# A one-core hybrid decoder layer on TensorE: twelve multiplications of ones put into a wait of the first tile, and the outputs of a tile's first two chunks formed together

## The reference

```python
h = rmsnorm(x, g_pre_mix)
z, q, k, v, glow, og = jnp.split(h @ w_in, SPLIT_IDX, axis=-1)
gk = jax.nn.log_sigmoid((glow @ w_gk2 + b_gk2).astype(jnp.float32)) / GLA_GATE_NORMALIZER
pool_out, pool_new = pool_mixer(z, pool_buf, start, w_pool, pool_scale)
gla_out, gla_new = gla_mixer(q, k, v, gk, og, gla_state, gla_norm)
mix = jnp.concatenate([pool_out.astype(x.dtype), gla_out.astype(x.dtype)], axis=-1) @ w_o
x = x + rmsnorm(mix, g_post_mix)
f, conv_new = conv_ffn(rmsnorm(x, g_pre_ffn), conv_buf, w_up, w_conv, b_conv, w_down)
x = x + rmsnorm(f, g_post_ffn)
x = x + (p.astype(x.dtype) @ w_ple) * jax.nn.sigmoid(x @ w_ple_gate)
```

```python
o_inter = jnp.einsum('bhtd,bhdv->bhtv', qc * jnp.exp(b), S)
o = o_inter + jnp.einsum('bhts,bhsv->bhtv', A, vc)
...
o = rmsnorm(o, gla_norm)
o = o.transpose(0, 2, 1, 3).reshape(B, L, GLA_VDIM) * jax.nn.silu(og.astype(f32))
```

## Time and profile before

| | us |
|---|---|
| median of 3 runs | 2523.79 (2523.52 to 2526.18) |
| the profiled execution, its own time | 2522.07 |
| its span in the trace | 2520.3 |
| PE busy | 2500.1 (99%) |
| DVE busy | 1592.6 (63%) |
| ACT busy | 1296.7 (51%) |
| POOL busy | 177.5 (7%) |
| TensorE clock granted, mean | 0.998 |

### The profile page before, as it was taken

How to read it: one execution, slowest core, us unless ns; L and a number is a source line. 1 busy time by engine, 2 the same in 40 slices (tenths; PEclk the granted TensorE clock), 3 DMA queues, 4 the chain that set the end, 5 groups by cost and what they waited for, 6 DMA issues and landing times.

```text
span 2520.3 us, 40462 instructions
## 1 busy us (share of the span) xinstructions
PE 2500.1 (99%) x16224; PEld 2432.9 (97%) x16224; DVE 1592.6 (63%) x2523; ACT 1296.7 (51%) x1989; POOL 177.5 (7%) x508
## 2 busy tenths in 40 slices
PE   9999999999999999999999999999999999999998
PEld 8889999989999999999999999999999999999998
DVE  6778765666665456666545666655566664667865
ACT  5455554564444456444445644444564444566554
POOL 4201000100000010000001000000100000010000
PEclk9999999999999999999999999999999999999999
DMA  8435556444444644544464544346454434656565
GB/s 249 133 127 165 172 150 234 143 159 147 153 127 124 223 144 166 153 154 123 126 217 152 167 150 152 122 130 215 151 167 151 142 123 129 204 186 209 190 181 182
DMA packets 120473, 409.08 MB, mean 162 GB/s; under 512 B 12896, under 2 KB 22496, under 8 KB 119776
## 3 DMA queue, kind: packets, MB, share of 16 engines
q1 hardware_dynamic: 120288, 406.51, 50.2%
HBM read 383.56 MB, written 22.89 MB: 161 GB/s over the span
## 4 chain that ended last, share of the span: by engine, by line
PE 97%; DVE 2%; ACT 1%; issue 1%; DMA 0%; DVEq 0%; POOL 0%; ACTq 0%; POOLq 0%
PE G L1628 29%; PE G L1630 29%; PE G L1629 29%; PE X L1674 2%; PE G L1907 1%; PE G L1908 1%; PE G L1909 1%; PE X L1624 1%; PE X L1732 1%; PE X L1738 0%; DVE w_lo L1128 0%; PE X L1791 0%; PE G L1870 0%; PE X L1653 0%; PE X L1717 0%
## 5 line engine op out<-in xcount | busy, mean ns | idle before, releaser
L1628 PE MATMUL G<-h_hi,w_hi 128*128 128x384 f32 (+2 forms) x3072 | 997.8, 325 | 6.0 <-DVE w_lo L1128 3.1
L1630 PE MATMUL G<-h_lo,w_hi 128*128 128x384 f32 (+2 forms) x3072 | 987.9, 322 | 0.0
L1629 PE MATMUL G<-h_hi,w_lo 128*128 128x384 f32 (+2 forms) x3072 | 987.8, 322 | 0.0
L725 ACT ACTIVATE w_hi<-stage 128x1024 fp32r<-128x1024 f32 (+1 forms) x505 | 524.1, 1038 | 416.2 <-DMA stage<-in_w_up_units_dram 243.5
L1128 DVE TENSOR_TENSOR w_lo<-stage,w_hi 128x1024 fp32r<-128x1024 f32 (+1 forms) x505 | 604.9, 1198 | 160.7 <-ACT w_hi L725 160.1
L1628 PEld LDWEIGHTS G<-h_hi,w_hi 128*128 128x128 f32 x3072 | 579.4, 189 | 14.4 <-DVE w_lo L1128 4.4
L1629 PEld LDWEIGHTS G<-h_hi,w_lo 128*128 128x128 f32 x3072 | 579.6, 189 | 1.5
L1630 PEld LDWEIGHTS G<-h_lo,w_hi 128*128 128x128 f32 x3072 | 579.3, 189 | 0.0
L1628 PE MATMUL G<-y_hi,w_hi 128*128 128x384 f32 (+2 forms) x1056 | 342.6, 324 | 0.0
L1630 PE MATMUL G<-y_lo,w_hi 128*128 128x384 f32 (+2 forms) x1056 | 339.4, 321 | 0.0
L1629 PE MATMUL G<-y_hi,w_lo 128*128 128x384 f32 (+2 forms) x1056 | 339.3, 321 | 0.0
(11 more groups left out here) (213 smaller groups left out, 2700.0 us busy)
## 6 DMA issues: line engine op xcount, KB each, us to landing
stage<-in_w_up_units_dram SPq DMA_DIRECT2D x264, 512.0 KB, 3.6
w_lo<-kept_lo SPq DMA_DIRECT2D x107, 512.0 KB, 4.7
stage<-in_w_down_units_dram SPq DMA_DIRECT2D x96, 448.0 KB, 3.3
w_whole<-in_w_in_units_dram SPq DMA_DIRECT2D x72, 512.0 KB, 3.8
stage<-in_w_o_units_dram SPq DMA_DIRECT2D x48, 512.0 KB, 3.5
stage<-in_w_down_units_dram SPq DMA_DIRECT2D x48, 512.0 KB, 3.5
w_whole<-in_w_gate_units_dram SPq DMA_DIRECT2D x35, 512.0 KB, 3.8
stage<-in_w_in_units_dram SPq DMA_DIRECT2D x24, 512.0 KB, 4.4
```

The costliest lines, as they stand in the source:

```text
L725: act.activation(w_hi[s][:, 0:parts, :], whole[:, 0:parts, :], ACT.Copy).then_inc(hi_made, 1)
L1628: pe.matmul(ps[:, 0:w], l_hi, r_hi[:, 0:w], start=start, stop=False)
L1629: pe.matmul(ps[:, 0:w], l_lo, r_hi[:, 0:w], start=False, stop=False)
L1630: return pe.matmul(ps[:, 0:w], l_hi, r_lo[:, 0:w], start=False, stop=stop)
```

## The change

Two edits. First, PE no longer forms chunk 0's output after unit in 13; it forms chunks 0 and 1 together after unit in 14, and ACT copies both out at its step 15. Chunk 2 stays where it was. Second, in tile 0 twelve multiplications of ones into the first bank of unit o 0 are issued between `pool_group` 3 and `spread_heads`.

```diff
@@ ACT @@
-                    if m in (14, 15):
-                        copy_out(t, m - 14)
+                    if m == 15:
+                        copy_out(t, 0)
+                        copy_out(t, 1)
@@ PE @@
-                    if 13 <= m < 13 + chunks(t):
-                        out_chunk(t, m - 13)
+                    if m == 14:
+                        out_chunk(t, 0)
+                        out_chunk(t, 1)
+                    if m == 15 and chunks(t) == 3:
+                        out_chunk(t, 2)
@@ PE, in the branch for m == 15 and t == 0 @@
                         pool_group(t, 2)
                         pool_group(t, 3)
+                        keep_warm(open_bank((0, "o", 0)), 12)
                         spread_heads(t)
```

## The result

| | kernel before | changed kernel |
|---|---|---|
| median of 22 runs each, us | 2525.14 | 2528.78 |
| lowest to highest, us | 2522.29 to 2532.25 | 2526.08 to 2532.70 |
| ratio, 95% interval | | 1.0013 [1.0008, 1.0019] |
| the profiled execution, its own time, us | 2522.07 | 2526.08 |
| its span, us | 2520.3 | 2524.4 |

The change makes the kernel 0.13% slower, 2.0 to 4.8 us by the interval. That is within the 0.2% called "no change" in the prediction, but the time lies above the predicted range of 2521.7 to 2527.3, and the difference of medians is 3.6 us where 0.8 was forecast.

What follows compares the result with a forecast made beforehand. PE was taken to bound the kernel, holding 97% of the chain of waits, with DVE's chain of heads setting unit o 0's end. Ones +0.8, clock 0, joining 0: 2523.79 + 0.8 = 2524.6 us, range 2521.7 to 2527.3.

Steps and rivals of the forecast that it cites:

- The ones' delay: Tile 0, ahead of `spread_heads`: twelve ones make it start 0.8 us late, low end 0.7, high end 1.2.
- the price of 0.11 us a record: Read from 40 records of ones in tile 0; the twelve multiplications are 24 records and take 2.63 us.
- A side remark: At half clock 56 records took 9.34 us, so 24 ones would take 4.0 us and delay 2.2; not taken.
- The joining: Chunks 0 and 1 together: saves 0, as one chunk's own records fill its 1.73 us; lower end -1.2 us.
- the copy's slack: Tile 0, ACT: chunk 0's copies end 0.8 us ahead of need by the samples' first output.
- The clock: Unit o 0's first twelve matmuls need 1.5 us less at 2.4 GHz, hidden by waits for DVE: 0, other end -1.5.
- The clock falls later: Rival: a fall behind PE's pauses ahead of the heads hits units o 1 and o 2, costing 1.5 us: 2526.1; chance 0.09.
- The pauses: Tile 0, unit o 0: after the ones PE idles 0.7 us or so ahead of heads 1, 2 and 3.
- The range: 2521.7 to 2527.3 us: from both gains together to the late clock with the ones' high price, and a little beyond.
- The base: Median of the runs shown, 2523.79 us, to which the forecast change of 0.8 us was added.

Runs made afterwards that it cites:

- the fills: Two more ones ahead of each of unit o 0's four head products: ratio 1.0002 with six ones in the kernel before, 1.0007 on the changed kernel.
- the first kernel with products in the wait: Kernel before with tile 0's units o 0 and o 1 side by side, their pool group 0 and 1 products in the wait: 2522.17 against 2525.58 us.
- the two forms of the pair: Kernel before with units o 0 and o 1 multiplied side by side, without or with ACT making unit o 2's high part earlier: ratios 0.9989 and 0.9985.

## Why the prediction was wrong

- *The ones' delay.* Forecast 0.8 us, measured 0.87. Right, by the price of 0.11 us a record; the ones took 2.83 us to the next matmul against 2.63 plus 0.1 for the change of form. A side remark, which the sum did not use, misread: in that trace only the first 28 of the 56 records lie 0.21 us apart, as at half clock, and the others 0.11, so that 24 at half clock would take 5.1 us and not 4.0. No trace has the ones of the wait at half clock.
- *The joining.* Forecast 0: a pair costs 3.47 us, twice 1.73, and alone it changes nothing (0.9998). Right, and so was the copy's slack. The price that was read off for one chunk already held no cost of entering or leaving.
- *The clock.* This is the step that failed: "What the ones give back is the clock ... I take 0 for it; the other end is -1.5." The first half was right, the fast clock of unit o 0's first products is eaten by the wait for DVE. But the term had another side that the bounds left out. It measured +2.8 us in the changed kernel's first trace. In the kernel before, the slow stretch beside the heads did two things at no price: it fell where PE was ahead of DVE anyway, and it stretched the products until the pauses between them were nearly gone (only one of 0.67 is left in the earlier trace rows). That this is what keeps a second fall away in the kernel before is argued from the traces; the fills test it from the other side. With the ones, PE is fast, three pauses of 0.63 to 0.68 us open within 3.5 us, and the clock falls behind them, where PE waits for nothing and every slow matmul is lost time.
- *The rival.* "The clock falls later" named this mechanism and its place, with a chance of 0.09 and a price of 1.5 us, taken from the length of the one slow stretch on show. In four traces it lasted 6.8 to 6.9 us. The pauses were foreseen and counted as idle time without a price. The chance was low because I took the late fall for a matter of luck, in which the ones have no part.
- *The range.* Its high end was the sum with 1.2 for the ones and 1.5 for the late clock, 2526.5, and a little more. With the measured 0.87 for the ones and 2.8 for the clock the sum is 2527.5; the rest up to 2528.78 is the base, next.
- *The base.* The three runs shown had a median of 2523.79, 22 have 2525.14. That shifts both kernels and explains 1.4 of the 4.2 us between forecast and result, none of the ratio. The other 2.8 are the clock.

What stays open: the traces show which pauses come ahead of the fall and that filling them keeps the clock up, with one trace of each kernel (two of the two main ones), while the times of the filled kernels are too scattered to confirm it. Why the late stretch lasts 6.8 us where others last 3.4 was not tried.

## What to carry to other kernels

Before warming PE through a wait, look at what lies behind it: a slow clock that falls beside an engine which sets the pace costs nothing, and taking it away there can bring it back where PE sets the pace. Here the ones were harmless only where the pauses that follow were filled too, and even then they gained nothing; filling the wait with products that are ready gained 3.4 us (0.5 to 5.1). And a price at which joining two interruptions can save anything is found by taking an interruption's own records from its cost; here nothing was left.

## What the runs showed of the hardware

The clock also fell where PE was busy nearly all the time. In the changed kernel's second trace it is 0.50 from 94.2 to 97.6, right behind the samples' outputs, small matmuls of 8 and 64 columns; in four other kernels it fell there too (92.8 to 94.1), with and without ones. The stages of the first kernel with products in the wait show PE busy for 3.34 of 3.40 us before the fall:

```profile
89.80:93.20 3.40, 3.34 (x43) 3.06 (x42) 3.33 (x12) 1.75 (x4) 0.00 (x0) 1.00 0.70 234
93.20:96.60 3.40, 3.40 (x15) 3.40 (x14) 0.78 (x1) 0.00 (x0) 0.00 (x0) 0.50 0.02 5
```

In the two forms of the pair it cost 1.5 us each. In two traces it fell again at 101, behind the samples' second outputs. In three traces the clock fell at about 65.5 us, right behind the scores (small matmuls as well). That it is the small matmuls that bring it down was not tested. So the same kernel loses the clock at different places from run to run, and the 22 runs of the kernel before are spread over 10 us. The Trainium skill ("TensorE: Matmul & The Clock Gate", "What's actually happening") has this as a monitor that runs free of the program. The traces fit that, with falls at 111.4 in one and at 94.2, 101.0 and 114.6 in the other trace of the same kernel.

Half clock is felt by `spread_heads` as well: 1.45 us instead of 0.82.
